# Two mixing tiles prepared inside the latent attention, the pooling stage in halves, and a reordered VectorE list in the mixers

## The chip, the cores and the metric

The kernel runs on one core of one Trainium2 chip. The metric is device time in microseconds (us) for one execution of the whole program, from the inputs in HBM to the output in HBM. A profile of one execution goes with the times.

## What is computed

The program is two blocks of a transformer, one behind the other, on one sequence of 1024 rows and 1024 columns in float32. The first block has differential attention, a mixture of experts, a pooling mixer and a second mixture of experts. The second block has two layers; each projects the rows, mixes them in three ways (retention, latent attention, gated linear attention), gates the three results, and multiplies them by an output matrix. The change touches the pooling mixer and the two layers of the second block:

```python
def pool_mixer(x, w_in, w_grp, ls, w_out):
    u = (x @ w_in).reshape(B, S, N_POOL_GROUPS, POOL_GROUP_DIM)
    for g, w in enumerate(POOL_WINDOWS):          # windows 2, 4, 8, 16
        cs = jnp.cumsum(u[:, :, g], axis=1)
        lag = jnp.pad(cs[:, :S - w], ((0, 0), (w, 0), (0, 0)))
        feats.append((cs - lag) / jnp.minimum(count, float(w))[None, :, None] - u[:, :, g])
    y = jnp.einsum('bsgc,gcd->bsgd', jnp.stack(feats, axis=2), w_grp).reshape(B, S, D_MODEL) * ls
    return y @ w_out

for l in range(DEPTH):                            # the second block
    shift, scale, gate = jnp.split(silu(c) @ ada_w[l] + ada_b[l], 3, axis=-1)
    proj = (rms_norm(x, norm_w[l]) * (1.0 + scale) + shift) @ w_in[l]
    r_o = rms_norm(retention(rope(rq), rope(rk), rv))
    m_o = mla(mq, mkv, mkr, ...)                  # latent attention
    g_o = rms_norm(gla(gq, gk, gv, gg, w_g2[l], b_g2[l]), gla_norm[l])
    x = x + gate * (concat([r_o * silu(rz), m_o * silu(mz), g_o * silu(gz)]) @ w_out[l])
```

## The kernel before, in words

The program is a row of phases. Each phase has its own tiles and semaphores, and each engine (PE is TensorE, DVE VectorE, ACT ScalarE, POOL GpSimd, SP the queue that issues most DMAs) works through a list written out by hand. Nothing reorders a list: an instruction that waits holds everything behind it on its engine.

**The pooling phase** (`phase_combine_pool`, tiles named `pool_...`). First the outputs of the experts are combined: for each of 8 row tiles, POOL gathers two rows per token, PE adds them with two diagonal matrices (`sums`, 4 products of 512 columns into `rp`), DVE adds the residual and takes statistics (`add`), POOL takes a power, DVE normalizes (`norm`), and PE turns the tile (`transposes`) into `pool_hT`. When all 8 tiles are turned, `channels(ct, c)` multiplies with the matrix `pool_w`, one block of 128 channels and one half of the rows at a time (8 products of 512 columns). ACT copies both halves into `pool_u`, `window(ct)` on DVE forms the moving means over all 1024 rows, and `outputs(g)` on PE multiplies a group of two blocks with `pool_wg`. Beside this DVE adds up 16 weighted chunks of `ada_w` (`m.add`, line 2175) for the modulation of both later layers; `m.total` on PE (line 2184) sums them over the partitions after the eighth and the sixteenth.

**The latent attention** (`phase_attention` with one map, tiles `mla_...`, once per layer). It has 32 steps, 4 per head; a step handles one long and one short row tile, 9 blocks of keys together. In step n PE forms the scores of step n+1 (lines 318 to 320), DVE masks them and takes their maxima, ACT takes the exponentials (line 936) and copies turned probabilities (line 931), and PE turns the probabilities (757) and multiplies them with the values (831). At the end of the phase ACT applies silu to the gates of two row tiles (`silus`).

**The mixing phase** (`phase_mix_out`, tiles `mixout_...`, once per layer). Per row tile i: `open_tile` turns the projected columns (PE), `copies` takes them out of PSUM (ACT), `gate_and_retention` forms the gate and the retention scores (PE), `gate_in`, `softplus`, `gate_sums` and `exponents` make the decay factors (DVE and ACT in turn), `gla_operands` multiplies them into queries and keys (DVE), then `gla_scores`, `updates` and `outputs` on PE, `gla_parts` and `states` on DVE, the normalization, `mixed_transposes`, and the output product `project` (48 products of 512 columns a tile). The output matrix is split in a high and a low part before its first use (`split_hi` on ACT, `split_lo` on DVE); 5 of its 8 chunks are loaded during the attention, the last 3 reuse the buffers of the first 3, so SP loads them when those have been split. `MixAhead` holds what is loaded during the attention. Tiles 0 and 1 are opened at the head of the phase, one behind the other:

```python
open_tile(0); keep_warm(nc, K, spare, 2)
gate_and_retention(0)
open_tile(1); keep_warm(nc, K, spare, 3)
gate_and_retention(1); keep_warm(nc, K, spare, 2)
gla_scores(0); updates(0)
```

## Time and profile before

| | us |
|---|---|
| median of 3 runs | 3649.71 (3647.54 to 3656.63) |
| the profiled execution, its own time | 3647.19 |
| its span in the profile | 3645.3 |
| PE busy | 3449.7 (95%) |
| DVE busy | 2415.8 (66%) |
| ACT busy | 1881.2 (52%) |
| POOL busy | 453.2 (12%) |

The span is what the profile covers; 1.9 us of the execution lie around it. PE busy counts pipelined products, so 95% is not the share in which PE works at its peak. TensorE's granted clock was 0.979 of full speed in the mean. A timeline row has its start, its length, the engine, the line, output and inputs, the count of records, and in brackets the idle time of the engine before it with what ended it. A float32 product shows as two records on PE.

### The profile page before, as it was taken

To read this page: it belongs to the slowest core of one execution; us is meant where nothing else is said; L and a number is where in the kernel's file an instruction comes from. 1 tells how busy PE (TensorE), PEld (TensorE's weight loads), DVE (VectorE), ACT (ScalarE), POOL (GpSimd) and SP (SyncE) were. 2 spreads that over 40 slices of the span, in tenths; PEclk is the share of its full clock that TensorE was granted. 3 is DMA by queue.
4 is the path that set the end of the run, shared out by engine and by line. 5 is a ranking of instruction groups with operands and counts; after the bars stand their busy time and mean duration, and the time that the engine had idled before them with its cause. 6 is when DMAs were issued, how large, how long until landed. Compare 5 with 4: busy or idle time off the path is not lost. (4 is left out here: it accounts for less than half of the span.)

```text
span 3645.3 us, 53840 instructions
## 1 busy us (share of the span) xinstructions
PE 3449.7 (95%) x18229; PEld 2681.6 (74%) x18229; DVE 2415.8 (66%) x3956; ACT 1881.2 (52%) x3175; POOL 453.2 (12%) x499
## 2 busy tenths in 40 slices
PE   8998889899999979998999999899998999999988
PEld 7885658688888835586888887487886767787766
DVE  3226877699988855647998887763176755407675
ACT  3215662288888720114888886232267733216674
POOL 0000002021111130000211111400001310000032
PEclk9999999899999999998999999999999999999999
DMA  6532224399999976444999998643232343424241
GB/s 247 218 146 94 81 90 170 112 392 381 376 374 378 348 263 233 166 177 166 384 379 378 378 370 302 239 173 122 98 91 84 110 144 124 157 70 129 70 127 64
DMA packets 413217, 766.16 MB, mean 210 GB/s; under 512 B 107609, under 2 KB 162545, under 8 KB 411000
## 3 DMA queue, kind: packets, MB, share of 16 engines
q1 hardware_dynamic: 390008, 711.93, 54.6%
q0 software_dynamic: 22752, 50.93, 3.8%
q8 instruction: 106, 1.74, 0.2%
q10 hardware_dynamic: 288, 1.05, 0.1%
q14 instruction: 63, 0.52, 0.0%
HBM read 643.00 MB, written 152.72 MB: 218 GB/s over the span
## 5 line engine op out<-in xcount | busy, mean ns | idle before, releaser
L253 DVE TENSOR_TENSOR experts_gate_lo<-weights_gate,experts_gate_hi 128x1024 fp32r<-128x1024 f32 x256 | 302.9, 1221 | 84.2 <-ACT experts_gate_hi L249 83.5
L249 ACT CAST experts_gate_hi<-weights_gate 128x1024 fp32r<-128x1024 f32 x256 | 257.4, 1056 | 131.8 <-DMA weights_gate<-in_moe_w_gate_dram 97.5
L253 DVE TENSOR_TENSOR experts_down_lo<-weights_down,experts_down_hi 128x1024 fp32r<-128x1024 f32 x256 | 296.1, 1219 | 27.2 <-ACT experts_down_hi L249 27.2
L253 DVE TENSOR_TENSOR experts_up_lo<-weights_up,experts_up_hi 128x1024 fp32r<-128x1024 f32 x256 | 295.9, 1218 | 0.3
L318 PE MATMUL project_acc<-project_wh,project_hh 128*128 128x512 f32 (+2 forms) x768 | 285.9, 372 | 0.0
L320 PE MATMUL project_acc<-project_wh,project_hl 128*128 128x512 f32 (+2 forms) x768 | 281.9, 367 | 0.0
L319 PE MATMUL project_acc<-project_wl,project_hh 128*128 128x512 f32 (+2 forms) x768 | 281.8, 367 | 0.0
L249 ACT CAST experts_up_hi<-weights_up 128x1024 fp32r<-128x1024 f32 x256 | 257.4, 1057 | 13.6 <-DMA weights_up<-in_moe_w_up_dram 11.6
L249 ACT CAST experts_down_hi<-weights_down 128x1024 fp32r<-128x1024 f32 x256 | 254.7, 1053 | 8.8 <-DMA weights_down<-in_moe_w_down_dram 8.6
L2780 ACT COPY project_row<-project_acc 128x512 f32<-128x512 f32 (+2 forms) x96 | 51.8, 540 | 363.6 <-PE project_acc L320 363.6
L318 PE MATMUL experts_gp<-experts_gate_hi,experts_xh 128*128 128x512 f32 x512 | 201.7, 394 | 12.5 <-DVE experts_xl L253 12.2
L318 PE MATMUL experts_yp<-experts_down_hi,experts_hTh 128*128 128x512 f32 x512 | 204.6, 400 | 2.7 <-DVE experts_hTl L253 2.7
L318 PE MATMUL experts_up<-experts_up_hi,experts_xh 128*128 128x512 f32 x512 | 204.9, 400 | 0.0
L320 PE MATMUL experts_up<-experts_up_hi,experts_xl 128*128 128x512 f32 x512 | 200.2, 391 | 0.0
L319 PE MATMUL experts_up<-experts_up_lo,experts_xh 128*128 128x512 f32 x512 | 199.8, 390 | 0.0
L320 PE MATMUL experts_gp<-experts_gate_hi,experts_xl 128*128 128x512 f32 x512 | 199.6, 390 | 0.0
L319 PE MATMUL experts_yp<-experts_down_lo,experts_hTh 128*128 128x512 f32 x512 | 199.6, 390 | 0.0
L320 PE MATMUL experts_yp<-experts_down_hi,experts_hTl 128*128 128x512 f32 x512 | 199.5, 390 | 0.0
L319 PE MATMUL experts_gp<-experts_gate_lo,experts_xh 128*128 128x512 f32 x512 | 199.4, 390 | 0.0
L1772 POOL DMA_INDIRECT scratch_y<-experts_y,experts_at x62 | 83.5, 1346 | 633.2 <-ACT experts_y L1892 633.2
L319 PEld LDWEIGHTS project_acc<-project_wl,project_hh 128*128 128x128 f32 x768 | 144.8, 189 | 20.3 <-issue 0.5
L318 PEld LDWEIGHTS project_acc<-project_wh,project_hh 128*128 128x128 f32 x768 | 144.9, 189 | 20.1 <-issue 0.5
(551 smaller groups left out, 8308.7 us busy)
## 6 DMA issues: line engine op xcount, KB each, us to landing
weights_gate<-in_moe_w_gate_dram SPq DMA_DIRECT2D x256, 512.0 KB, 12.0
weights_up<-in_moe_w_up_dram SPq DMA_DIRECT2D x256, 512.0 KB, 13.4
weights_down<-in_moe_w_down_dram SPq DMA_DIRECT2D x256, 512.0 KB, 11.5
scratch_y<-qkv_zero SPq DMA_DIRECT2D x48, 512.0 KB, 4.5
pool_shared<-in_ada_w_dram SPq DMA_DIRECT2D x16, 1536.0 KB, 6.7
scratch_proj<-project_row SPq DMA_DIRECT2D x64, 256.0 KB, 2.0
head_store<-in_attn_w_qkv_dram SPq DMA_DIRECT2D x48, 256.0 KB, 3.7
scratch_qkv<-qkv_row SPq DMA_DIRECT2D x48, 256.0 KB, 2.1
```

The costliest lines, as they stand in the source:

```text
L249: return act.copy(hi, src)
L253: return dve.tensor_tensor(lo, src, hi.bitcast(F32), ALU.subtract)
L318: nc.tensor.matmul(acc, a[0][k], b[0][k], start=(start and k == 0), stop=False)
L319: nc.tensor.matmul(acc, a[0][k], b[1][k], start=False, stop=False)
L320: last = nc.tensor.matmul(acc, a[1][k], b[0][k], start=False, stop=(stop and k == n - 1))
L1772: pool.indirect_dma_start(out=y, out_offset=bass.IndirectOffsetOnAxis(ap=at[:, u, :], axis=0), in_=ysb[:, u, :], in_offset=None, bounds_ch ...
L2780: act.copy(row[:, n % SLOTS, 0:width(s)], acc[:, n % AB, 0:width(s)]).then_inc(acc_done, 1)
```

## The change

It has three parts, and no constant or computed value differs.

1. **Tiles 0 and 1 of each mixing phase are prepared in the attention before it.** The tiles of data and the semaphores that this needs move from `phase_mix_out` into `MixAhead`, and one more PSUM bank (`first`) is taken in the attention. At the end of a step, PE turns (steps 16 and 17 for tile 0, 24 and 25 for tile 1) and forms gate and retention scores (18, 26); ACT copies (16, 17 and 24, 25), takes the softplus (19, 27) and the exponents (21, 29); DVE takes the gate in (18, 26), sums it (20, 28) and forms the operands of tile 0 (22, 23). POOL clears `rqm` and forms the decayed queries and keys of both tiles during the attention. The mixing phase begins with `gla_scores(0)`; it keeps 6 warming products where it had 12.
2. **The pooling phase works in two halves of 512 rows.** `channels(0)` starts when four row tiles are turned; the turns of tiles 4 to 7 stand between the products. The groups come in the order of windows 16, 8, 4, 2 for each half, the last 16 columns of a block are kept in `tails` for the second half, and `pool_u`, `pool_s`, `pool_pT` and `pool_y` are halved and doubled in number. `pool_w` is loaded in four pieces by group of columns (rows of 1 KB each) instead of eight by rows (4 KB). Tiles 4 to 7 of the combination use two PSUM banks instead of four. The stores of y are eight of half the size.
3. **In the mixing phase DVE forms the gated operands of tile i+1 before the residual of tile i-1.**

```diff
@@ phase_attention, step n @@
+                    if prefetch:
+                        prefetch.first_on_pe(nc, pe, K, first, n)
                     a_wait(n, 1)
...
+                    if prefetch:
+                        prefetch.first_on_act(act, K, first, n)
...
+                    if prefetch:
+                        prefetch.first_on_dve(dve, first_ch, K, first, n)
@@ MixAhead @@
+    FIRST = (16, 24)
+    def first_on_pe(self, nc, pe, K, bank, n):
+        for i, at in enumerate(self.FIRST):
+            if n == at:
+                if i > 0:
+                    pe.wait_ge(self.ar_ready, i)
+                self.turn_front(nc, pe, K, bank, i)
+            if n == at + 1:
+                pe.wait_ge(self.t_copied, 2 * i + 1)
+                self.turn_back(nc, K, bank, i)
+            if n == at + 2:
+                pe.wait_ge(self.t_copied, 2 * i + 2)
+                pe.wait_ge(self.small_in, 48)
+                self.gate_and_retention(nc, bank, i)
+    def first_on_act(self, act, K, bank, n):
...
+            if n == at:
+                self.copy_front(act, bank, i)
+            if n == at + 1:
+                self.copy_back(act, K, bank, i)
+            if n == at + 3:
+                self.softplus(act, i)
+            if n == at + 5:
+                self.exponents(act, i)
@@ phase_mix_out, PE @@
-                open_tile(0)
-                keep_warm(nc, K, spare, 2)
-                gate_and_retention(0)
-                open_tile(1)
-                keep_warm(nc, K, spare, 3)
-                gate_and_retention(1)
-                keep_warm(nc, K, spare, 2)
                 gla_scores(0)
                 updates(0)
-                keep_warm(nc, K, acc[1][:, :], 5)
+                keep_warm(nc, K, acc[1][:, :], 4)
+                outputs(0)
                 gla_scores(1)
-                outputs(0)
                 open_tile(2)
+                keep_warm(nc, K, acc[1][:, :], 2)
                 updates(1)
@@ phase_mix_out, DVE, tile i @@
                         gated(i)
+                    if has(i + 1):
+                        gla_operands(i + 1)
+                    if final and has(i - 2):
+                        final_mean(i - 2)
...
                     if has(i - 1):
                         residual(i - 1, 0)
-                    if has(i + 1):
-                        gla_operands(i + 1)
-                    if final and has(i - 2):
-                        final_mean(i - 2)
@@ phase_combine_pool, PE @@
+                for i in range(HT):
+                    cb.sums(nc, pe, i + 2)
                     transposes(i)
+                for n in range(2):
+                    channels(n)
+                    cb.sums(nc, pe, n + 2 + HT)
+                    transposes(n + HT)
+                for G in range(GROUPS_):
+                    if G + 1 < GROUPS_:
+                        channels(CG * (G + 1))
+                    if G == GROUPS_ - 1:
+                        m.total(nc, pe, 1, mod_bank)
+                    outputs(G)
+                    if G < 1:
+                        transposes(TILES - 2)
+                    if G == 4:
+                        m.total(nc, pe, 0, mod_bank)
...
```

On ACT in the first latent attention, at the end of step 19, the list before ran from the exponentials of one step to the copies of the next (`mla_narrow` and `mla_wide` are the probabilities of the short and the long tile):

```order
L936 ACTIVATE mla_narrow,totals<-mla_s,mla_bias 128x128
L931 COPY mla_aT<-mla_tp 128x512
L936 ACTIVATE mla_wide,totals<-mla_s,mla_bias 128x896
L931 COPY mla_aT<-mla_tp 128x512
L927 ACTIVATE mla_qh<-mla_tp 96x512
```

and runs now (`ahead_ab` and `ahead_sg` belong to the softplus of tile 0):

```order
L944 ACTIVATE mla_narrow,totals<-mla_s,mla_bias 128x128
L3098 ACTIVATE ahead_ab<-ahead_ab 128x128
L3100 ACT_TABLE_LOAD
L3100 ACTIVATE ahead_sg<-ahead_ab 128x128
L939 COPY mla_aT<-mla_tp 128x512
L944 ACT_TABLE_LOAD
L944 ACTIVATE mla_wide,totals<-mla_s,mla_bias 128x896
L939 COPY mla_aT<-mla_tp 128x512
L935 ACTIVATE mla_qh<-mla_tp 96x512
```

Two activations and two table loads now stand between the short tile's exponentials and the long tile's of the next step.

On PE at the head of each mixing phase the list before was (`mixout_pf<-constants` are warming products):

```order
L3207 MATMUL mixout_tA<-constants,ahead_row 128x128 x4
L3209 MATMUL mixout_tB<-constants,ahead_row 128x128
L3210 MATMUL mixout_tB<-constants,ahead_row 128x128
L3211 MATMUL mixout_tB<-constants,ahead_row 16x128
L328 MATMUL mixout_pf<-constants 128x512 x2
L3221 MATMUL mixout_sc<-mixout_ggT,ahead_g 128x128
L3224 MATMUL mixout_sc<-mixout_rqm,mixout_rkT 64x128 x4
```

and is now:

```order
L3432 MATMUL mixout_sc<-constants,ahead_kwT 128x128
L3437 MATMUL mixout_pf<-ahead_qpos,ahead_kneg 64x256 x2
L3437 MATMUL mixout_pf<-ahead_qneg,ahead_kpos 64x256 x2
L3452 MATMUL mixout_u<-ahead_vv,ahead_rkw 128x128 x4
L3455 MATMUL mixout_u<-ahead_vv,mixout_kw 128x256 x2
L328 MATMUL mixout_acc<-constants 128x512 x4
L3465 MATMUL mixout_u<-mixout_s_r,ahead_rqw 64x64 x8
```

The phase starts with the scores of tile 0, whose operands were made in the attention.

On PE in the pooling phase, from the turns of the last combined tiles on, the list before was (`pool_tp` turned tiles, `pool_up` channels, `pool_rp` outputs):

```order
L2312 MATMUL pool_tp<-constants,pool_hn 128x128 x16
L2323 MATMUL pool_up<-pool_hT,pool_w 128x512 x8
L2312 MATMUL pool_tp<-constants,pool_hn 128x128 x8
L2323 MATMUL pool_up<-pool_hT,pool_w 128x512 x40
L2335 MATMUL pool_rp<-pool_wg,pool_pT 128x256 x16
```

and is now, from the turn of tile 3 on:

```order
L2358 MATMUL pool_tp<-constants,pool_hn 128x128 x8
L2372 MATMUL pool_up<-pool_hT,pool_w 128x512 x8
L2094 MATMUL pool_rp<-pool_shared,pool_diag 128x512
L2095 MATMUL pool_rp<-pool_shared,pool_diag 128x512
L2094 MATMUL pool_rp<-pool_shared,pool_diag 128x512
L2095 MATMUL pool_rp<-pool_shared,pool_diag 128x512
L2358 MATMUL pool_tp<-constants,pool_hn 128x128 x8
L2372 MATMUL pool_up<-pool_hT,pool_w 128x512 x8
```

The first channels now follow the fourth turned tile, and the sums and turns of later tiles stand behind them.

## Rows read from the trace of the kernel before

**Rows 1.** Head of the page: the span of the profiled execution

```profile
span 3645.3 us, 53840 instructions
```

**Rows 2.** Busy time in two stretches: inside the first attention, first mixing phase

```profile
2714.00:2733.00 19.00, 18.70 (x170) 16.30 (x170) 14.86 (x36) 13.01 (x31) 0.00 (x0) 1.00 0.29 70
...
2787.00:2976.00 189.00, 172.42 (x1297) 125.92 (x1296) 122.93 (x257) 111.76 (x231) 51.45 (x44) 0.96 0.31 104
```

**Rows 3.** Timeline of the pooling phase, PE

```profile
1335.94 1.10 PE L2312 MATMUL pool_tp<-constants,pool_hn 128*128 128x128 f32 x8 [1.73 <-DVE pool_hn L1156]
...
1357.65 9.18 PE L2323 MATMUL pool_up<-pool_hT,pool_w 128*128 128x512 f32 x16 [2.71 <-issue]
...
1403.04 7.07 PE L2335 MATMUL pool_rp<-pool_wg,pool_pT 128*128 128x256 f32 x32
...
1409.95 27.63 PE L2323 MATMUL pool_up<-pool_hT,pool_w 128*128 128x512 f32 x64
...
1437.41 7.57 PE L2184 MATMUL pool_tp<-pool_ones,pool_ada_sum 128*128 128x1 f32 x48
...
1444.84 10.02 PE L2335 MATMUL pool_rp<-pool_wg,pool_pT 128*128 128x256 f32 x32
...
1520.53 0.27 PE L2206 MATMUL pool_tp<-constants,pool_mod_cols 128*24 128x128 f32 x1
```

**Rows 4.** Groups by line: the additions for the modulation

```profile
L2175 DVE SCALAR_TENSOR_TENSOR pool_ada_sum<-pool_shared,pool_c,pool_ada_sum 128x3072 f32<-128x3072 f32 x14 | 47.9, 3419 | 10.5 <-DMA pool_shared<-in_ada_w_dram 9.7
```

**Rows 5.** Timeline of the head of the first mixing phase

```profile
2789.41 0.63 PE L3207 MATMUL mixout_tA<-constants,ahead_row 128*128 128x128 f32 x4 [1.12 <-PEq L707]
...
2805.14 0.33 PE L3233 MATMUL mixout_sc<-constants,mixout_kwT 128*128 128x128 f32 x1 [1.15 <-DVE mixout_qpos L3490]
...
2812.16 4.63 DVE L253 TENSOR_TENSOR mixout_w_lo<-ahead_raw,mixout_w_hi 128x1024 fp32r<-128x1024 f32 x4
...
2812.57 0.27 PE L3233 MATMUL mixout_acc<-constants,mixout_kwT 128*128 128x128 f32 x1
...
2813.68 0.64 PE L3266 MATMUL mixout_u<-mixout_s_r,mixout_rqw 128*64 128x64 f32 x16
...
2821.61 2.94 ACT L249 CAST mixout_w_hi<-ahead_raw 128x1024 fp32r<-128x1024 f32 x3 [0.84 <-DMA ahead_raw<-in_w_out_dram]
...
2830.28 0.80 PE L3302 MATMUL mixout_acc<-mixout_w_hi,mixout_mh 128*128 128x512 f32 x1 [2.81 <-DVE mixout_ml L253]
```

**Rows 6.** Timeline of a later tile of the first mixing phase, PE

```profile
2878.43 0.60 PE L3207 MATMUL mixout_tA<-constants,ahead_row 128*128 128x128 f32 x4
...
2879.11 0.48 PE L3302 MATMUL mixout_acc<-mixout_w_hi,mixout_mh 128*128 128x512 f32 x1
...
2882.31 0.33 PE L3233 MATMUL mixout_sc<-constants,mixout_kwT 128*128 128x128 f32 x1 [0.18 <-DVE mixout_qpos L3490]
...
2884.11 0.51 PE L3302 MATMUL mixout_acc<-mixout_w_hi,mixout_mh 128*128 128x512 f32 x1
...
2887.11 0.48 PE L3221 MATMUL mixout_sc<-mixout_ggT,ahead_g 16*128 16x128 f32 x2
...
2888.39 0.69 PE L3266 MATMUL mixout_u<-mixout_s_r,mixout_rqw 128*64 128x64 f32 x16 [0.20 <-DVE mixout_s_g L3511]
```

**Rows 7.** Waits of PE in the second mixing phase: total, times, longest

```profile
PE mixout_u L3253 <- DVE mixout_kw L3496: 8.4, 6, 1.7
```

**Rows 8.** Timeline of one step of the first attention, ACT and PE

```profile
2712.09 0.59 ACT L931 COPY mla_aT<-mla_tp 128x512 f32<-128x512 f32 x1 [0.90 <-PE mla_tp L757]
...
2712.89 1.01 ACT L936 ACTIVATE mla_wide<-mla_s,mla_bias 128x896 f32<-128x896 f32 x1 [0.21 <-DVE mla_bias L1023]
...
2714.53 0.48 PE L318 MATMUL mla_s<-mla_kh,mla_qh 96*128 96x512 f32 x1
```

**Rows 9.** Timeline of the mixing phase, ACT: the softplus of tile 0

```profile
2797.02 1.28 ACT L3383 ACT_TABLE_LOAD   x1
...
2798.31 0.31 ACT L3383 ACTIVATE mixout_sg<-mixout_ab 128x128 f32<-128x128 f32 x1
```

More of the change, by code:

```diff
@@ L666, in phase_attention @@
         o_ps = ph.ps("o_ps", [P, 2, HALF // 2])
+        first = ph.ps("first", [P, 4, P]) if prefetch else None
         if not diff:
@@ L2439, in adds, with norm @@
-                def adds(ct):
-                    for n in range(sum(ADDS[:ct]), sum(ADDS[:ct + 1])):
-                        m.add(dve, n)
-                dve.wait_ge(small_in, 16 * (2 * NG + 1))
-                for ct in range(CG):
-                    window(ct)
-                    adds(ct)
-                for g in range(NG):
-                    outputs(g)
-                    if g + 1 < NG:
-                        for ct in range(CG * (g + 1), CG * (g + 2)):
-                            window(ct)
-                            adds(ct)
+                def norm(i):
+                    cb.norm(dve, cch, i, (tp_ready, 2 * (i - 2) + 2))
@@ new lines, in adds @@
+                def adds(k):
+                    for n in range(sum(ADDS[:k]), sum(ADDS[:k + 1])):
+                        m.add(dve, n)
+                cb.add(dve, cch, 0)
+                for i in range(1, HT + 2):
+                    cb.add(dve, cch, i)
+                    norm(i - 1)
+                dve.wait_ge(small_in, 16 * (2 * NG + 1))
+                for n in range(2):
+                    window(n)
+                    cb.add(dve, cch, n + HT + 2)
+                    norm(n + HT + 1)
@@ L2456, in phase_project @@
+                for G in range(GROUPS_):
+                    outputs(G)
+                    for n in range(CG * (G + 1), min(CG * (G + 2), STEPS)):
+                        window(n)
+                        if n == CG:
+                            norm(TILES - 1)
+                        adds(n)
 def phase_project(nc, K, name, x, w_in, q_norm, w_uq, kv_norm, w_ukv, mod, tabs, proj, mq, mk, mkv, head, experts=None):
@@ new lines, in gate_and_retention @@
+    def gate_and_retention(self, nc, bank, i):
+        nc.tensor.matmul(bank[:, 3, :], self.g2[:, :], self.ggT[:, i % 2, :], start=True, stop=True)
+        for p in range(2):
+            for c in range(2):
+                t = slice(c * CH, (c + 1) * CH)
+                last = nc.tensor.matmul(bank[t, p, :].rearrange("p (h c) -> p h c", h=2), self.rkT[:, i % 2, p, t],
+                                        self.rqm[:, i % 2, 2 * p:2 * p + 2, t], start=True, stop=True)
+        last.then_inc(self.rs_ready, 1)
@@ new lines, in copy_front, with copy_back @@
+    def copy_front(self, act, bank, i):
+        act.wait_ge(self.t_ready, 2 * i + 1)
+        for h in range(2):
+            r = slice(RD * h, RD * h + RD)
+            act.copy(self.rqm[r, i % 2, h::2, :], bank[r, 0:2, :])
+        act.copy(self.rkT[:, i % 2, :, :], bank[:, 2:4, :]).then_inc(self.t_copied, 1)
+    def copy_back(self, act, K, bank, i):
+        act.wait_ge(self.t_ready, 2 * i + 2)
+        act.copy(self.ggT[:, i % 2, :], bank[0:GRANK, 2, :])
+        act.copy(self.gkT[:, i % 2, :], bank[:, 1, :])
+        for h in range(GH):
+            last = act.activation(self.gqm[:, i % 2, h, :], bank[:, 0, :], ACT.Copy, scale=K["ghead"][:, h:h + 1])
+        last.then_inc(self.t_copied, 1)
@@ new lines, in softplus, with exponents @@
+    def softplus(self, act, i):
+        ch = Chain(act, self.act_own, i)
+        act.wait_ge(self.ab_ready, i + 1)
+        ch(act.activation(self.ab[:, :], self.ab[:, :], ACT.Exp, scale=-1.0))
+        ch.wait()
+        act.activation(self.sg[:, :], self.ab[:, :], ACT.Ln, bias=1.0).then_inc(self.sg_ready, 1)
+    def exponents(self, act, i):
+        act.wait_ge(self.cum_ready, i + 1)
+        act.activation(self.epos[:, :], self.cum[:, :], ACT.Exp, scale=1.0 / 16)
+        act.activation(self.eneg[:, :], self.cum[:, :], ACT.Exp, scale=-1.0 / 16)
+        for c in range(2):
+            t = slice(c * CH, (c + 1) * CH)
+            act.activation(self.el[:, t], self.cum[:, t], ACT.Exp, scale=-1.0 / 16, bias=self.last2[:, c:c + 1])
+        act.activation(self.elast[:, i % 2, :], self.last2[:, :], ACT.Exp).then_inc(self.exps_ready, 1)
@@ L2970, in load_w, with first_on_pool @@
+    def first_on_pool(self, pool, K):
+        pool.memset(self.rqm[:, :, :, :], 0.0).then_inc(self.rqm_zero, 1)
+        pool.wait_ge(self.rqm_zero, 1)
+        for i in range(2):
+            self.decayed_queries(pool, K, i)
+            self.decayed_keys(pool, K, i)
     def load_w(self, sp, n):
@@ L3576, in _ @@
                 gla_operands(1)
-                for n in range(4):
-                    split_lo(n)
+                split_lo(0)
                 gla_parts(1)
+                split_lo(1)
                 mean_squares(0)
@@ L3582, in _ @@
                 states(1)
+                split_lo(2)
                 normalized(0)
-                for n in range(4, KC):
+                for n in range(3, KC):
                     split_lo(n)
```

521 lines of the change are left out of this document (267 added, 254 removed).

## The prediction

> **What bounds the kernel now.** First the head of the page and its engine table: the span is 3645.3 us [rows 1], and PE counts as busy for 95% of it, DVE 66%, ACT 52%. So PE is where time is won or lost, in three ways: its gaps, products that it is given or spared, and its clock. The windows say how full it is where the change works. In the attention PE is busy for 18.70 of 19.00 us and in the first mixing phase for 172.42 of 189, at a mean clock of 0.96 [rows 2]. The attention has hardly a gap to put new work in; the mixing phase has 16.6 us without work, and more that only looks like work (warming products, pipelined products whose operands came late).
>
> Then the timelines. In the pooling phase the reader is to see how long PE goes from the turns of tile 3 to the first products (1335.94 to 1357.65), and that it ends on the turn of the last total at 1520.53 [rows 3]. In the head of the mixing phase two tiles are opened one behind the other on three engines by turns, and the first scores come 15.7 us after the first turn [rows 5]. Rows 6 and 7 are small waits of PE for DVE that come back tile by tile.
>
> All sums are against the profiled execution, 3647.19 us, which is 2.5 below the median of the runs; the forecast adds this back.
>
> **The heads of the mixing phases.** From 2789.41 to 2805.14 PE turns, copies are taken and factors made, and only then do `gla_scores(0)` run [rows 5]. All of that leaves the phase: at most 15.7 us per phase. It isn't all won, since the output product needs the three chunks of the output matrix that are reloaded. Before, three `split_lo` of 4.63 / 4 = 1.16 each are done at 2812.16 + 3.5 = 2815.6; the last chunk has landed at 2821.61, 6.0 later; the first product of `project` starts at 2830.28, another 8.7 later [rows 5]. Counted from the first turn (T) it starts at T + 40.9. After, DVE has in its order the parts and states of tile 0, the operands of tile 1, and the three splits with the parts and states of tile 1 and the normalization between them. With the durations of the same phase I get the third split done at T + 16.5 (an estimate, from a list of some 25 rows). The chunk lands 4 to 6 later, and with 8.7 to the first product that is T + 29.2 to 31.2. The gain is 9.7 to 11.7; I take 10.7, twice: **-21.4**. Bounds for each head: 15.7 if all is won, 5 if a chunk lands as much later as three splits (3.5) and a wait as that of [rows 5] for `ml` (2.8) make it. On SP the loads of the chunks stand where they did.
>
> **VectorE's reordered list.** In tiles past the first, PE's scores take 1.80 (2882.31 to 2884.11) after a wait of 0.18 for `qpos`, where the same scores take 1.11 (2812.57 to 2813.68) when operands are there [rows 5, 6]. With operands made first, 0.69 + 0.18 = 0.87 goes in 6 tiles: -5.2. In the second mixing phase PE waits 8.4 us in 6 times for `kw`, which the same function makes [rows 7]: -8.4. The residual that now comes later frees the accumulator later; its next user is the project of the tile after, several us away, so this costs nothing unless that cover goes, and then up to the 0.87 again. Sum **-13.6**; bounds -17 (the clock gains a little as well) and -8 (`kw` alone).
>
> **The pooling phase.** Before, 1335.94 to 1520.53 is 184.6 us. I rebuild it from rows. The copies of tile 3 I put at 2.0 from the start of its turns, to 1337.9 (0.55 for the first half of the turns of 1.10, and two copies of 0.59 as in [rows 8], with a little between). Eight products take 27.63 / 4 = 6.91, sixteen times: 110.5. Half of a group's outputs takes 7.07 / 2 = 3.54, eight times: 28.3. Two totals of 7.57: 15.1. Four turned tiles of 1.10: 4.4. The sums of tiles 6 and 7 are four products of 512 columns each, 3.45: 6.9. After a total the outputs took 10.02 instead of 7.07, at a lower clock: 2 times 2.95 is 5.9 [rows 3]. One stall stays, about 1.4, where outputs wait for a window behind an addition of 3.42 for the modulation [rows 4]. Together 1337.9 + 172.5 = 1510.4: **-10.1**. What goes is the stretch up to 1357.65, where PE idles between sums and turns. The split itself adds no product; it adds instructions on DVE and ACT, at sizes of half. Bounds: -18 (no stall, clock up throughout, 7.3 less) and +5: the loads of `pool_w` in pieces of 1 KB or the windows, now twice as often, hold the products for 15 us. For the second, ACT must refill a block every 6.91 us and DVE form a window in the same time, beside 3.42 per addition.
>
> **What the attention pays**, per layer. PE gets all that the head gave up except warming: the turns of a tile, 2878.43 to 2879.11, 0.68, and gate and retention scores, 2887.11 to 2888.39 less a wait of 0.20, 1.08 [rows 6]. That is 1.76 a tile, 3.5 for two; there is no cover, since PE has 0.30 free in 19.00 [rows 2]. ACT is tight at one point in a step: it copies (0.59 after 0.90 idle), takes the long tile's exponentials (1.01 after 0.21 idle), which end at 2713.90, and PE's next step begins at 2714.53, 0.63 later [rows 8]. The slack is 0.90 + 0.21 + 0.63 = 1.74. The softplus puts two activations of 0.31 and a table load of 1.28 there [rows 9], and another load before the exponentials, 3.2 in all: some 1.6 are left over and pass to PE, 3.2 for two tiles. The other pieces on ACT (copies, exponents) and on DVE I put at 1.0 to 1.6 each, two to four instructions of 0.3 to 0.6 as in [rows 8, 9], and so about the size of the slack; for them, for what is queued behind them and for POOL's share of the memory I take 0.7 a tile. 3.5 + 3.2 + 1.4 = 8.1 a layer, **+16.2** for both. Bounds: 7 (PE's work alone) and 26 (every piece a half us over, ten pieces a layer).
>
> What was PE's at the head counts as removed above, so nothing is counted twice. POOL's pieces, `rqm` and the decayed queries, have six steps until they are read and cost nothing unless the cover of some 28 us fails; then their waits return at the head.
>
> **Sum**: -21.4 - 13.6 - 10.1 + 16.2 = -28.9, which is 3618.3 in the profiled execution's terms and 3620.8 in the median's; I give 3620.
>
> A rule that speaks against the change: the softplus' loads are 1.28 from start of the load to start of the activation (2797.02 to 2798.31), with no gap between them [rows 9]. The Trainium skill, "ScalarE: Activation LUTs", section "What ACT_TABLE_LOAD costs", puts a drain of about 1380 ns beside the 1283 ns of the load, some 2.66 us a switch. By it the sum would be 11 us higher (8 loads more in the attentions, 1.38 each), an estimate by that page. By the row the sum stands as it is.
>
> **The rivals.**
> - *Every piece in the attention costs double.* Speaks for it: 18.70 of 19.00 [rows 2] and the 0.21 of ACT [rows 8]. Against: exponentials of short tiles leave gaps elsewhere in a step. 12 more: 3632. Chance 0.17.
> - *The pooling phase gains nothing*, since windows of half length and loads hold the products. For it: 9.7 of DVE's 10.5 us idle before the additions wait for their DMA [rows 4]. 10 more: 3631. Chance 0.12.
> - *All goes better*: the pooling gains 18 and an attention pays only 4 a layer: 8 + 8 less, 3604. Chance 0.11.
> - *A table load drains ACT.* Eight loads in the two attentions, each with a stop of its own length (1.28, [rows 9]) on ACT while exponentials wait: 8 x 1.28 = 10 more, 3630. The row shows load and activation back to back. The Trainium skill has the rule (named above). Chance 0.03.
> - *The other side, slower.* The steps have no slack where the pieces fall, and each delay on ACT and DVE passes whole to PE, because the scores of step n+1 wait for exponentials that wait in turn. The work of two tiles was a chain of 15.7 at the head [rows 5]; it comes whole in the attention instead, with two table loads a tile more to get back to the exponentials' function (4 x 1.28 = 5.1, [rows 9]): 20.8 a layer, 41.6 for both. Against it stand heads of 2 x 5, a list of 8 and a pooling phase at +5, the lower ends: 41.6 - 10 - 8 + 5 = +28.6, 3678. With the gains at these ends (13) the program is slower by over 11 from an attention cost of 24 on, with those of the forecast (45.1) from 56 on. For it speaks the 0.30 of [rows 2]; against it the 1.74 of [rows 8]. Chance 0.04.
>
> The forecast itself has 0.53. That the change doesn't do what it says is excluded: the instruction lists show the moved pieces.
>
> **Numbers.** About 0.3%, 11 us, is what a measurement of this kernel can tell from no change, so faster means below 3638.8. The forecast, the first four rivals and most of their own spread lie below: 0.90. Within: 0.06, slower 0.04. The range 3602 to 3638 takes in the rivals at 3604, 3631 and 3632 with a spread; what is left out is the slower side and combinations of two misses.
>
> **What would show it.** In the profile after: the attentions longer by about 8 us each, with PE's waits for `mla_wide` in steps 20 and 28; first product of `project` at some T + 30 behind the first scores; no waits of PE for `qpos` and `kw` in the mixers; the pooling phase 10 shorter, with PE's first channels right behind the fourth turned tile, and clock dips only at the two totals. The prediction is wrong if an attention grows by over 15, if a mixing phase shrinks by under 12, or if PE in the pooling phase waits for windows at each half group.

## The result, and the profile after

The changed kernel takes 3607.87 us (median of 4 runs, 3605.45 to 3610.51), beside 3649.43 for the kernel before: 41.6 us less, a ratio of 0.9883 (95% interval 0.9866 to 0.99). The forecast was 3620, and the range from 3602 to 3638 holds the time. The time is 12 us below the forecast, and the phases tell where. They are read from one profiled execution of each kernel; that of the kernel before lies 2.2 us under its median and that of the changed one 0.6 over, so the spans differ by 38.7 and the medians by 41.6.

The first row of each phase on PE gives the length of the phase, from its start to that of the next. First the timeline of PE before, then the same of the kernel after (start, length, engine and line, output and inputs):

```profile
1293.35 7.11 PE L328 MATMUL pool_up<-constants 128*128 128x512 f32 x16 [1.36 <-PEq L1723]
...
1526.97 2.81 PE L328 MATMUL out_lg<-constants 128*128 128x512 f32 x6 [2.74 <-PEq L2253]
...
2627.89 2.21 PE L810 MATMUL mla_s<-keep 96*128 96x512 f32 x6 [1.05 <-DVE mla_nothing L1073]
...
2978.71 1.89 PE L328 MATMUL project_lp<-constants 128*128 128x512 f32 x3 [2.06 <-PEq L3086]
...
3284.89 2.18 PE L810 MATMUL mla_s<-keep 96*128 96x512 f32 x6 [0.75 <-DVE mla_nothing L1073]
...
3447.82 0.63 PE L3207 MATMUL mixout_tA<-constants,ahead_row 128*128 128x128 f32 x4 [1.14 <-PEq L707]
```

```profile
1292.78 7.11 PE L328 MATMUL pool_up<-constants 128*128 128x512 f32 x16 [1.35 <-PEq L1736]
...
1509.48 2.81 PE L328 MATMUL out_lg<-constants 128*128 128x512 f32 x6 [1.33 <-PEq L2290]
...
2611.60 2.18 PE L816 MATMUL mla_s<-keep 96*128 96x512 f32 x6 [0.75 <-DVE mla_nothing L1084]
...
2779.59 0.30 PE L3432 MATMUL mixout_sc<-constants,ahead_kwT 128*128 128x128 f32 x1 [1.37 <-PEq L708]
...
2952.46 7.94 PE L328 MATMUL project_lp<-constants 128*128 128x512 f32 x14 [2.06 <-PEq L3309]
...
3260.16 2.17 PE L816 MATMUL mla_s<-keep 96*128 96x512 f32 x6 [0.77 <-DVE mla_nothing L1084]
...
3428.21 0.30 PE L3432 MATMUL mixout_sc<-constants,ahead_kwT 128*128 128x128 f32 x1 [1.39 <-PEq L708]
```

Read as differences (the first mixing phase before starts in [rows 5] at 2789.41; the spans end at 3645.3 and 3606.6):

| phase | before | after | difference | the forecast's |
|---|---|---|---|---|
| pooling | 233.6 | 216.7 | -16.9 | -10.1 |
| first attention | 161.5 | 168.0 | +6.5 | +8.1 |
| first mixing | 189.3 | 172.9 | -16.4 | -15.9 |
| second attention | 162.9 | 168.0 | +5.1 | +8.1 |
| second mixing | 197.5 | 178.4 | -19.1 | -19.1 |
| all other phases | | | +2.1 | 0 |
| span | 3645.3 | 3606.6 | -38.7 | -28.9 |

The forecast's figures for a mixing phase are its head, 10.7, with 5.2 and 8.4 for the list of VectorE. The phases that the change does not touch differ by up to 1.7 us each between the two traces. The pooling phase can be read less finely: this kernel and the ten runs further down that have the same code for it give 214.2 to 217.9.

**The pooling phase after**, timeline of PE, for [rows 3]:

```profile
1335.40 1.09 PE L2358 MATMUL pool_tp<-constants,pool_hn 128*128 128x128 f32 x8 [1.13 <-DVE pool_hn L1169]
1337.31 7.10 PE L2372 MATMUL pool_up<-pool_hT,pool_w 128*128 128x512 f32 x16 [0.82 <-ACT pool_hT L2430]
...
1366.61 3.62 PE L2386 MATMUL pool_rp<-pool_wg,pool_pT 128*128 128x256 f32 x16
1370.06 1.04 PE L2358 MATMUL pool_tp<-constants,pool_hn 128*128 128x128 f32 x8
1370.93 7.03 PE L2372 MATMUL pool_up<-pool_hT,pool_w 128*128 128x512 f32 x16
...
1423.37 13.90 PE L2372 MATMUL pool_up<-pool_hT,pool_w 128*128 128x512 f32 x32
1437.10 3.66 PE L2386 MATMUL pool_rp<-pool_wg,pool_pT 128*128 128x256 f32 x16
1440.60 6.08 PE L2204 MATMUL pool_tp<-pool_ones,pool_ada_sum 128*128 128x1 f32 x48
1446.54 16.67 PE L2372 MATMUL pool_up<-pool_hT,pool_w 128*128 128x512 f32 x32
1463.05 3.62 PE L2386 MATMUL pool_rp<-pool_wg,pool_pT 128*128 128x256 f32 x16
...
1490.67 8.16 PE L2204 MATMUL pool_tp<-pool_ones,pool_ada_sum 128*128 128x1 f32 x48
1498.70 5.91 PE L2386 MATMUL pool_rp<-pool_wg,pool_pT 128*128 128x256 f32 x16
1504.44 0.27 PE L2226 MATMUL pool_tp<-constants,pool_mod_cols 128*24 128x128 f32 x1
```

The first products start 1.9 us behind the turn of the fourth tile, where they started 21.7 behind it, and from there to 1504.44 no row has a wait. In five of those ten other runs one or two of 0.3 to 0.8 us are left there, for a window. Outside the totals themselves, the lower clock is left in two places of this stretch, behind the totals: 16.51 us from start to start for 32 records that take 13.73 elsewhere, and 5.74 for outputs that take 3.5. Ahead of the fourth turn it shows as before, there in rows of 1.9 to 2.0 us at 1316.85 for sums that take 1.0 elsewhere.

**The mixing phases after.** The waits of PE from 2779.5 to 2952 (reason: total, times, longest):

```profile
PE mixout_acc L3501 <- DVE mixout_ml L253: 4.5, 1, 4.5
PE mixout_tA L3488 <- issue: 3.0, 1, 3.0
PE mixout_tA L3063 <- DMA ahead_row<-scratch_proj: 2.4, 1, 2.4
PE mixout_u L3465 <- DVE mixout_s_g L3644: 2.2, 6, 1.2
...
PE mixout_u L3452 <- DVE mixout_kw L3629: 0.4, 1, 0.4
```

The waits for `qpos` are gone and one of 0.4 for `kw` is left, in both mixing phases. All that is left of size lies in the head:

```profile
2799.73 0.63 PE L3488 MATMUL mixout_tA<-constants,mixout_mixed 128*128 128x128 f32 x4 [3.04 <-issue]
...
2802.27 2.94 ACT L249 CAST mixout_w_hi<-ahead_raw 128x1024 fp32r<-128x1024 f32 x3 [7.16 <-DMA ahead_raw<-in_w_out_dram]
...
2808.93 0.80 PE L3501 MATMUL mixout_acc<-mixout_w_hi,mixout_mh 128*128 128x512 f32 x1 [4.48 <-DVE mixout_ml L253]
```

What comes before the reload, on PE and then on DVE, where the third split of the output matrix is the last row:

```profile
2791.90 0.66 PE L3063 MATMUL mixout_tA<-constants,ahead_row 128*128 128x128 f32 x4 [2.40 <-DMA ahead_row<-scratch_proj]
...
2795.73 0.61 DVE L3643 SCALAR_TENSOR_TENSOR mixout_s_r<-mixout_s_r,constants,mixout_u 128x128 f32<-128x128 f32 x2 [2.59 <-PE mixout_u L3455]
...
2797.80 1.23 DVE L253 TENSOR_TENSOR mixout_w_lo<-ahead_raw,mixout_w_hi 128x1024 fp32r<-128x1024 f32 x1
```

The product with the output matrix starts 29.3 us behind the first scores (2779.59), where it started 40.9 behind the first turn: 11.5 less. ACT waits 7.2 us for the reloaded chunks, and the mixed rows stand behind them. The head also runs in part at the lower clock: over the 30 us from 2799.59 the granted clock is 0.83, which the forecast had not named.

**The attention after.** ACT around step 19, for [rows 8], and PE behind it:

```profile
2715.61 0.31 ACT L3098 ACTIVATE ahead_ab<-ahead_ab 128x128 f32<-128x128 f32 x1
2715.94 1.28 ACT L3100 ACT_TABLE_LOAD   x1
2717.24 0.31 ACT L3100 ACTIVATE ahead_sg<-ahead_ab 128x128 f32<-128x128 f32 x1
2717.45 0.57 ACT L939 COPY mla_aT<-mla_tp 128x512 f32<-128x512 f32 x1
2718.04 1.28 ACT L944 ACT_TABLE_LOAD   x1
2719.33 1.01 ACT L944 ACTIVATE mla_wide<-mla_s,mla_bias 128x896 f32<-128x896 f32 x1
...
2720.48 0.50 PE L318 MATMUL mla_s<-mla_kh,mla_qh 96*128 96x512 f32 x1 [1.18 <-ACT mla_wide L944]
```

From 2715.61 to the exponentials ACT has no gap, and PE waits 1.18. In each attention PE waits 2.5 us in 2 times in this way, and the new work on PE is 3.5 by the forecast, 6.0 together. The exponentials of the long tiles, compared one by one from the start of the attention, show the same: behind the fifth step, the attentions grow by 6.1 and 6.0. What is left of the differences in the table comes from the start, where PE waits for the keys by DMA: in the first attention it is 0.4 later by the fifth step, in the second 0.9 earlier, since before PE waited 2.1 us there and then had a clock of 0.57 for 4 us (from 3289.90), and after it has 1.00 there. The change does not touch this. The other pieces show no wait of their own: beside the two for the softplus and those for the keys, PE's waits sum to 4.1 us in the first attention where they were 4.9, and to 4.4 in the second where they were 3.4, with the more in its first 10 us.

### The profile page after: what moved, and what is told of

Read it like the earlier page. It is cut to its first block and busy times, and to the rows that moved or that the text cites. A ratio compares the mean times of both kernels' runs of the same rounds, so it can differ in the third digit from the quotient of the medians.

```text
span 3606.6 us, 53860 instructions
## 1 busy us (share of the span) xinstructions
PE 3428.8 (95%) x18205; PEld 2678.3 (74%) x18205; DVE 2410.1 (67%) x3983; ACT 1873.4 (52%) x3187; POOL 430.8 (12%) x499
## 5 line engine op out<-in xcount | busy, mean ns | idle before, releaser
L320 PEld LDWEIGHTS project_acc<-project_wh,project_hl 128*128 128x128 f32 x768 | 145.2, 189 | 20.5
```

The costliest lines, as they stand in the source:

```text
L320: last = nc.tensor.matmul(acc, a[1][k], b[0][k], start=False, stop=(stop and k == n - 1))
```

## The experiments

**The three parts apart.** Three kernels, each the kernel before with one part of the change, whose diff is the one shown ahead of the prediction. Expected of the pooling phase in halves:

> The kernel before with part 2 alone (the pooling phase in halves). Theory, that the three parts act apart from one another and the profile after shows each one's share: the pooling phase, first product to first product of the next phase, is 217 us long where it was 234, nothing else moves, and the program takes 17 us less than before (3632). Rival, that part of these 17 us came from the other parts, as by the buffers and memory of the later phases: less than 12.

Of the two tiles prepared in the attention:

> The kernel before with part 1 alone (two tiles prepared in each attention). Theory: heads and attentions as in the changed kernel, that is an attention of 168 us (6.5 and 5.1 more) and a first product of the output matrix 29 us behind the first scores, where it was 41 behind the first turn; per mixing phase 11.5 less; in all 23 - 11.6 = 11.5 us less than before (3638). Rival, that the heads gain more than that because the list of VectorE alone (part 3) gives less than 13.6: mixing phases of 174 and 180 us already here, 24 us less in all.

Of VectorE's reordered list:

> The kernel before with part 3 alone (operands of the next tile ahead of the residual on VectorE). Theory: no waits of PE for qpos and kw from the third tile on; 5 us less in the first mixing phase and 8.4 in the second, 13.6 in all (3636). Rival, that the wait only passes to the accumulator, which the residual frees later, or to the next normalization: under 5 us less in all, with new waits of PE for xn or for mixed.

All three ran beside the same runs of the kernel before (3650.47). Lengths by the first rows of the phases:

| | median | ratio | pooling | attentions | mixing phases |
|---|---|---|---|---|---|
| halves alone | 3631.92 | 0.9951 (0.9937 to 0.9966) | -16.8 | +0.8, +0.4 | 0, -1.3 |
| preparation alone | 3641.27 | 0.9978 (0.9969 to 0.9988) | +1.2 | +6.1, +5.1 | -11.8, -8.4 |
| list alone | 3633.79 | 0.9957 (0.9943 to 0.9971) | +1.1 | 0, +0.3 | -6.3, -10.5 |

The parts act apart as far as this can tell: the pooling phase has its whole gain alone, and -18.6, -9.2 and -16.7 make -44.5 where the whole has -41.6; by the intervals each of the three is known to 3 to 5 us. The preparation, the largest part of the diff, gives the least: 20.2 us off the mixing phases, 11.2 back on the attentions. The list alone, four moved lines of code, gives 16.8. The rival of the preparation (mixing phases of 174 and 180 already here) falls: they are 177.5 and 189.1, and the second gained 3 us less than its theory said. The rival of the list falls too; the wait does not pass to the accumulator.

**What the softplus costs in the attention.** In place of the logarithm a second exponential, so that no table is switched (the decay factors of these tiles are then others, and so is the output):

```diff
             if n == at + 3:
-                self.softplus(act, i)
+                self.softplus(act, i, ACT.Exp)
```

> The changed kernel with a second exponential in place of the logarithm in the softplus of tiles 0 and 1 in the attentions, so that no table is loaded there (the decay factors of these tiles are then others; nothing else differs). Theory, that a tile's two table loads (2.56 us) and two activations (0.6) stand against a slack of about 2 us on ACT, and PE waits 1.2 us for the rest: without the loads PE's waits for mla_wide in these steps go, each attention is 2.5 us shorter (165.5), the program 5. Rival, that PE waits there for something else, as for the banks or for VectorE: the attentions stay within 1 us.

And once more as much behind it:

```diff
             if n == at + 3:
                 self.softplus(act, i)
+                act.activation(self.epos[:, :], K["ident"], ACT.Exp)
+                act.activation(self.eneg[:, :], K["ident"], ACT.Ln, bias=1.0)
```

> The changed kernel, and behind the softplus of each of tiles 0 and 1 in the attentions an exponential and a logarithm on ACT once more with two further table loads, 3.2 us that nothing uses. Theory, that the slack of this step is used up: all 3.2 pass to PE, four times, each attention is 6.4 us longer (174.4), the program 12.8. Rival, that half of it is still hidden (PE catches up in later steps): under 3.5 us per attention. If a switch had a stop beside its load, it would show as more than 3.2 a tile.

Without the switch the attentions are 165.2 and 164.8 us long, 2.8 and 3.3 less than in the changed kernel, and PE's waits for `mla_wide` in these steps are gone. That confirms the term: a softplus costs PE 1.4 to 1.6 us, all of it by the two loads. The time was 3597.53 (one run), 10 us less than the changed kernel's and not 5; the attentions have 6.1 of that, and another 2.5 stand in the pooling phase, whose code is the same.

With it twice the attentions are 179.6 and 178.8 long, 11.6 and 10.8 more, and the time is 3627.59 (one run): not 3.2 a tile but 5.6 in the mean. Neither theory nor rival had that. ACT's timeline has the added pieces back to back:

```profile
2717.28 0.31 ACT L3100 ACTIVATE ahead_sg<-ahead_ab 128x128 f32<-128x128 f32 x1
2717.61 1.28 ACT L3181 ACT_TABLE_LOAD   x1
2718.91 0.31 ACT L3181 ACTIVATE ahead_epos<-constants 128x128 f32<-128x128 f32 x1
2719.22 1.28 ACT L3182 ACT_TABLE_LOAD   x1
2720.51 0.31 ACT L3182 ACTIVATE ahead_eneg<-constants 128x128 f32<-128x128 f32 x1
```

So a stop beside the load is not what the 2.4 us more are. PE's timeline and the windows of this kernel have the rest (a window's columns: length, busy time with instructions of PE, PEld, DVE, ACT and POOL, granted clock, share of the DMA engines, GB/s):

```profile
2721.44 0.30 PE L763 MATMUL mla_tp<-constants,mla_narrow 128*128 128x128 f32 x1 [2.20 <-ACT mla_aT L939]
2723.76 0.50 PE L318 MATMUL mla_s<-mla_kh,mla_qh 96*128 96x512 f32 x1 [2.02 <-ACT mla_wide L944]
...
2724.46 0.63 PE L320 MATMUL mla_s<-mla_kh,mla_ql 96*128 96x512 f32 x1
```

```profile
2718.00:2724.00 6.00, 1.78 (x18) 1.19 (x14) 1.12 (x4) 5.94 (x9) 0.00 (x0) 1.00 0.00 1
2724.00:2728.00 4.00, 4.00 (x18) 3.66 (x17) 3.08 (x8) 2.25 (x7) 0.00 (x0) 0.57 0.02 4
...
2768.00:2775.00 7.00, 6.31 (x30) 5.59 (x32) 2.81 (x7) 3.71 (x10) 0.00 (x0) 0.54 0.01 2
```

These are the first tile of the first attention and, in the last line, the stretch behind the second. The waits of the first are 2.20 and 2.02 where the changed kernel has one of 1.18: 3.0 more, the added time (the second tile has 2.48 and 2.02, 3.2 more). Behind them the clock is 0.57 for 4 us, near the lower of the two levels (1.2 GHz), and the products take 0.63 where they take 0.40; in the changed kernel the same stretch has 1.00. Four us at 0.57 lose 1.7, and seven at 0.54 lose 3.2. By the exponentials compared one by one with the changed kernel's, the first tile costs 4.4 and the second 6.3 us, and in the second attention 5.3 and 5.1; the 0.9 and 0.4 that are left of the differences arose at the start of the attentions, ahead of any softplus. For the first attention that is 3.0 and 1.7 against 4.4, and 3.2 and 3.2 against 6.3. So the slack was used up, as the theory had it, and what goes beyond the added 3.2 is the clock.

**The same work two steps later.**

```diff
-    FIRST = (16, 24)
+    FIRST = (18, 26)
```

> The changed kernel with both tiles prepared two steps later (from steps 18 and 26), so that the softplus falls in steps 21 and 29, where ACT turns no queries or keys beside it and the long tile's exponentials are shorter by 0.2. Theory, that the slack on ACT of the step decides what the softplus costs: PE's wait is about half of the 1.25 us, each attention 1 to 1.5 us shorter (166.8). Rival, that the slack is the gap between two exponentials (1.8 us in both places): within 0.4 us.

The attentions are 168.2 and 168.4 long, the time is 3609.8 (one run). The rival had the number right: no shorter. Its reason, the same slack in both places, is not what the waits show: the one for `mla_wide` behind the first tile is 0.9 where it was 1.2, and the second tile has one of 1.6 for a copy (`mla_aT`) where it had 1.3 for `mla_wide`, 2.5 together as in the changed kernel. No third place was tried.

**What holds the head now.** Five kernels show it in three steps. The edits are abridged: the conditions that keep a moved call from being made again in the loop behind it, and the places that calls were moved from, are left out. First the mixed rows of tile 0 ahead of the reloaded chunks:

```diff
 @@ ACT @@
                 copies(2)
+                mixed_his(0)
                 for n in range(5, KC):
                     split_hi(n)
 @@ DVE @@
-                for n in range(3, KC):
+                split_lo(3)
+                split_lo(4)
+                mixed_lo(0, 0)
+                mixed_lo(0, 1)
+                for n in range(5, KC):
                     split_lo(n)
```

> The changed kernel, and in the head of the mixing phases ACT and VectorE split the mixed rows of tile 0 before the three reloaded chunks of the output matrix, so that its product can start on the five chunks that are there. Theory, that the head is now held by the reload alone (ACT waits 7.2 us for it, PE 4.5 and 5.5 for the split rows behind it): the product starts as PE is through with the outputs of tile 1, 4.5 us sooner, at 25 behind the first scores, and each phase ends 3 to 4.5 us sooner, 6 to 9 in all (3600). Rival, that PE then waits inside the product for the low parts of the reloaded chunks, or that what is behind (the gate of tile 2 on ACT and VectorE) comes late instead: under 2 us in all.

The product starts 26.8 us behind the first scores, 2.5 sooner, and in the second mixing phase 25.0, 5.2 sooner; yet the phases are 175.4 and 178.4 long, 2.5 longer than in the changed kernel and as long as there. The rival's mechanism holds. In the first mixing phase:

```profile
PE mixout_sc L3432 <- DVE ahead_qpos L3139: 2.1, 1, 2.1
```

The wait of 4.5 is gone, one of 2.1 for `qpos` of tile 2 is new, and from 2795 to 2825, 20 to 50 us into the phase, the clock is 0.78 where the changed kernel has 0.83. The median, 3600.69 (ratio 0.9865, 0.9849 to 0.9881), lies 7 us below the changed kernel's all the same. The profile doesn't show why: it is of the slowest of the four executions, 3605.87, only 2.6 below the changed kernel's, and 2.0 of that stand in the pooling phase, whose code is the same. So this gain isn't explained by its mechanism.

Second, also row tile 2 loaded first and the gate and softplus of tile 2 early:

```diff
 @@ SP @@
+                load_row(2)
                 load_mo(0)
 @@ ACT @@
                 mixed_his(0)
+                ahead.softplus(act, 2)
 @@ DVE @@
-                states(1)
                 split_lo(2)
+                split_lo(3)
+                states(1)
                 normalized(0)
+                ahead.gate_in(dve, ch, sc, 2)
+                retention_scores(2)
+                split_lo(4)
+                mixed_lo(0, 0)
+                mixed_lo(0, 1)
+                ahead.gate_sums(dve, K, ch, 2)
```

> The changed kernel with another order in the head of the mixing phases: SP loads row tile 2 first; VectorE splits chunks 2 and 3 before the states of tile 1, and takes the gate of tile 2 in right after the normalization of tile 0; ACT and VectorE split the mixed rows of tile 0, and ACT takes the softplus of tile 2, before the reloaded chunks. Theory, that the run before this one failed because the gate of tile 2 stood behind the reloaded chunks, and PE waited 2.1 and 1.1 us for its operands and then ran at the lower clock: with both early, the product starts 22 to 23 us behind the first scores, no wait for qpos and kw follows, and each phase is 4 to 6 us shorter than in the changed kernel (168 and 173), 8 to 12 in all (3597). Rival, that the lower clock in the head takes most of it again: under 3 in all.

And then the same with four warming products ahead of the turns of the mixed rows:

```diff
                 gate_and_retention(2)
+                keep_warm(nc, K, acc[1][:, :], 4)
                 mixed_transposes(0)
```

> The same as head_order, and four warming products (1.9 us) on PE ahead of the turns of the mixed rows of tile 0, where PE waits about 2 us. Theory, that the lower clock behind the gaps of the head costs 2 us or more per phase: the clock stays up from there and the phases are 1 to 3 us shorter than in head_order. Rival, that the clock falls all the same or the products only take the place of the wait: within 1 us, or longer by what the products exceed the wait.

They take 3598.08 (0.9865, 0.9849 to 0.9882) and 3597.90 (0.9861, 0.9845 to 0.9878). Their product starts 24.1 and 21.9 us behind the first scores; the mixing phases are 172.8 and 174.7 long, then 168.8 and 173.8. The first mixing phase gained nothing from the order alone (the second 3.7), where the theory had 4 to 6 in each, and PE's wait of 2.2 for `qpos` stayed. With the warming products the first gained 4.0 and the second 0.9. The windows from 2790 to 2820 of both, the one without them first:

```profile
2790.00:2820.00 30.00, 23.89 (x171) 18.62 (x173) 20.44 (x43) 21.73 (x39) 10.09 (x9) 0.75 0.40 132
```

```profile
2790.00:2820.00 30.00, 25.05 (x232) 17.13 (x231) 22.92 (x48) 22.75 (x41) 11.40 (x10) 1.00 0.43 137
```

The clock is 0.75 and 1.00. The wait of 3.9 us ahead of the turns is 0.3, since the warming products take 3.70 there (not the 1.9 that the expectation had), while the waits of 2.3 for `qpos` and 1.6 for `kw` behind it are in this kernel too. So the theory of the clock holds for this place in these two traces, though the medians of the two kernels can't be told apart; the profiled execution with the warming products is the fastest of its four.

Third, the operands of tile 2, for which PE still waited 2.3, formed at once:

```diff
 @@ ACT @@
                     split_hi(n)
+                ahead.exponents(act, 2)
                 silus(2)
 @@ DVE @@
                     split_lo(n)
+                gla_operands(2)
```

> The same as head_warm, and in the head ACT takes the exponents of tile 2 before the silu of tile 2 and the outputs of tile 1, and VectorE forms the operands of tile 2 right after the last split. Theory, that PE's waits for qpos (2.3) and kw (1.6) in the head came from the exponents standing behind the silu and the copies of the outputs on ACT (5.3 us of them): these waits go, and each mixing phase is 2 to 4 us shorter than in head_warm (168.8 and 173.8), 4 to 8 in all (3592). Rival, that the outputs of tile 1, 2.6 us later on ACT, hold the normalization of tile 1 and with it the turns of its mixed rows: PE waits there instead, and it is within 2 us in all.

And then its scores (`gla_parts`) too:

```diff
                         mean_squares(i)
+                        if i == 1:
+                            gla_parts(2)
                         gated(i)
```

> The same as head_operands, and VectorE takes the scores and the key factors of tile 2 (kw) right behind the mean squares of tile 1, ahead of the residual and the normalization, which waits for POOL's power. Theory, that the wait of 3.3 us for kw in head_operands goes and half of it comes back as a wait for the mixed rows of tile 1: mixing phases of 168 and 173.5 us, 4 us less in all than head_operands and no more than 1 less than head_warm (3597). Rival, that the whole wait comes back one step on: as head_operands (3601).

They take 3602.19 (0.9869, 0.9853 to 0.9886) and 3599.19 (0.9857, 0.9841 to 0.9874). The mixing phases of the first are 170.1 and 175.7 long, 1.3 and 1.9 more than with the warming products alone, where the theory had 2 to 4 less. The wait for `qpos` is gone, but that for `kw` has grown from 1.6 to 3.3:

```profile
PE mixout_u L3452 <- DVE mixout_kw L3633: 3.7, 2, 3.3
```

As the rival had it, the normalization of tile 1 comes late, with the outputs of tile 1 later on ACT. PE meets this sooner than the rival said, at `kw`, which stands behind that normalization on VectorE. In the second kernel the wait is gone, with one of 2.5 for the mixed rows of tile 1 behind it:

```profile
PE mixout_tA L3488 <- issue: 2.8, 2, 2.5
```

Its mixing phases are 168.2 and 173.4 long, 0.5 and 0.4 below those of the kernel with the warming products, as its theory had them (168 and 173.5), and the time is 2 us above its 3597. What PE waits for now is the chain of tile 1 (outputs, squares, POOL's power, normalization); no kernel was built to shorten it.

**The changed kernel beside the last one.**

> The changed kernel once more, beside head_parts on one chip. Theory: 3608 within 3 us, that is 10 above head_parts. If the kernels with another head were only faster by the chip they ran on, it would be within 4 of head_parts.

It takes 3607.54 (3604.61 to 3611.51; ratio 0.9883, 0.9867 to 0.99) and the kernel beside it 3599.19 (3597.56 to 3600.33). The difference of 8.4 us stands on one chip, and no execution of the one reaches the other's. So the last kernel beats both kernels of this case. The kernel with the warming products ran beside the kernel before on another chip; its four executions (3594.82 to 3600.10) lie below all of the changed kernel's too.

## Why the prediction was right, and by how much it missed

- **The heads.** Predicted 9.7 to 11.7 each, taken 10.7, with the product at T + 29.2 to 31.2. It starts at T + 29.3. The preparation alone took 11.8 and 8.4 off the mixing phases, the second below the range. That the reload of the last chunks binds, and not the whole 15.7, was the step that mattered, and ACT's wait of 7.16 for them shows it. The exact hit is partly luck, since terms missed both ways: the third split is done at T + 19.4 and not 16.5, because VectorE waits 2.59 for the updates of tile 1, which stand on PE behind a wait of 2.40 for row tile 2; the chunks are there 3.2 later and not 4 to 6, at T + 22.7; and from there to the product it is 6.7 and not 8.7.
- **VectorE's list.** Predicted -13.6; alone it took 6.3 and 10.5 off, 16.8 in all, near the end of -17. Both waits went as said; the gain beyond them isn't traced.
- **The pooling phase.** Predicted -10.1, measured -16.9: the term that missed most, near its end of -18 (the other traces of the same code would give -15.7 to -19.4). The mechanism was right. From the turn of the fourth tile to the turn of the last total it has 169.0 us where the sum had 174.5. The largest single cause is the reading of lengths: a row's length holds the tail of its last product, which the next row's products overlap. 7.07 / 2 = 3.54 for an output is 3.46 from start to start, 6.91 is 6.87, a turned tile is 0.87 and not 1.10; over 16 + 8 + 4 pieces that is 2.2. The totals took 13.97 and not 15.1 (1.1), the lower clock 5.1 and not 5.9 (0.8), and the stall of 1.4, which was put in without a row of its own, isn't there (0.4 to 1.4 us of waits for a window are left in five of the ten other traces). Another 1.4 came from the end of the phase, 5.0 us from the last turn to the next phase where it was 6.4 ([rows 3] to 1526.97), which the sum did not look at; all traces of the new code have 5.0 to 5.1 there.
- **The attentions.** Predicted +8.1 each, measured +6.5 and +5.1, of which the change made 6.1 and 6.0; the rest arose at the start, as said above. PE's own work (3.5) and the softplus (3.2 taken, 2.5 measured in waits, 2.8 to 3.3 by taking its loads away) hold. The 0.7 a tile for all the other pieces failed: no row shows a wait from them. They were put at 1.0 to 1.6 each, smaller than the slack of 1.7, and only the piece that is larger than it shows a cost.
- **The table loads.** By the rule of the Trainium skill, "ScalarE: Activation LUTs", section "What ACT_TABLE_LOAD costs", that a switch drains for about 1380 ns beside the load, the sum would have been 11 us higher, an estimate by that page. The trace does not agree: around the softplus of tile 0, four loads in the kernel with the softplus twice and two in the changed one start within 0.02 us of the end of the instruction before, and the next instruction starts 1.29 to 1.30 after the load, in the full stream of the attention. The rival is dropped.
- **The rivals.** "Every piece costs double" falls by attentions of 6.5 and 5.1 more, and "the pooling phase gains nothing" by its 16.9. Of the case "all goes better" (pooling -18, an attention +4, 3604) the pooling half came true and half of the other. The slower side had the mechanism that the run with the softplus twice shows, delays on ACT passed whole to PE once the slack is gone; it needed a slack of nothing and there was about 1.7.

## What to carry to other kernels

When a list is rebuilt from rows of the trace, take durations from start to start of rows that follow one another without a wait, not their lengths; the difference was 0.04 to 0.2 us a piece and a third of the pooling phase's miss. Work moved beside a full engine cost here what exceeded the slack of the one step in which it fell, so compare each piece with that slack rather than charge all of them a little; and look at the order of the list on the engine that feeds the bound one: four moved lines gave more here than the largest part of the change. A wait that is taken away at the head of a chain pays only as far as the next piece is early too: that piece is worth naming before the edit. A single phase of a single trace moved by up to 3.7 us with the same code, so a gain of that size in one phase needs its own row to be believed.

## What was not expected of the hardware

Gaps of PE cost more than their length in these traces. In the attention two waits of 2.20 and 2.02 us within 5 us brought the granted clock to 0.57 for the 4 us behind them, while single waits of 1.18 left it at 1.00; in the head of the mixing phase waits of 3.9 us ahead of the turns, and of 2.2 and 1.2 later, went with 0.75 over 30 us, and warming products in the place of the first of them with 1.00. The kernels before and after have the lower clock in the head too, 0.83 over 30 us (from 2809.40 and from 2799.59). The forecast had the clock only behind the totals.
